# Fillers, load waits and the order of a few steps in a two-layer hybrid diffusion step

## The reference, cut to what matters

```
for l in range(2):
    sh1, sc1, ga1, sh2, sc2, ga2 = split(silu(cond) @ mod_w[l] + mod_b[l], 6)   # context and latent rows
    h = rms_norm(x, norm1_g[l]) * (1 + sc1) + sh1
    o = even_mixer(h) if l == 0 else odd_mixer(h)       # odd: Fourier mixer || 12-head latent attention
    x = x + ga1 * o
    h = rms_norm(x, norm2_g[l]) * (1 + sc2) + sh2
    g = argmax(group logits); e1, e2 = top2(expert logits within group g)
    x = x + ga2 * sum over e1, e2 of gate_e * (silu(h @ w1[e]) * (h @ w3[e])) @ w2[e]
y = rms_norm(x, final_norm_g)
# attention, per head: p = softmax(scale * (q_nope k_nope + q_pe k_pe)); out = p @ v
```

## Time and profile before

| | us |
|---|---|
| median of 3 runs (lowest, highest) | 779.63 (778.14, 781.07) |
| the profiled execution, whole | 773.11 |
| its span, first to last instruction | 771.3 |

### The profile page before, as it was taken

How to read it: one execution, slowest core, us unless ns; L and a number is a source line. 1 busy time by engine, 2 the same in 40 slices (tenths; PEclk the granted TensorE clock), 3 DMA queues, 4 the chain that set the end, 5 groups by cost and what they waited for, 6 DMA issues and landing times.

```text
span 771.3 us, 9539 instructions
## 1 busy us (share of the span) xinstructions
PE 694.5 (90%) x3655; PEld 388.2 (50%) x3655; DVE 244.7 (32%) x519; ACT 142.1 (18%) x290; POOL 170.8 (22%) x227
## 2 busy tenths in 40 slices
PE   1789999999999999799899998899799899999991
PEld 0335444554555665456445454355445556666650
DVE  0201212221155323223641323455221742323246
ACT  2101000000121212112121211355111121212211
POOL 5001011011331222212100210367404212222212
PEclk9899999999997999999989999999899899999996
DMA  9999999399356999996590582824410969979933
GB/s 329 393 359 308 400 386 365 110 419 425 165 204 250 400 419 421 420 421 249 199 410 8 207 357 110 332 105 157 144 55 28 358 259 416 419 302 423 384 136 131
DMA packets 53208, 219.46 MB, mean 285 GB/s; under 512 B 13774, under 2 KB 20942, under 8 KB 33969
## 3 DMA queue, kind: packets, MB, share of 16 engines
q1 hardware_dynamic: 31520, 178.59, 58.0%
q0 software_dynamic: 9664, 23.41, 8.1%
q10 hardware_dynamic: 11984, 16.92, 6.2%
HBM read 206.53 MB, written 20.68 MB: 295 GB/s over the span
## 4 chain that ended last, share of the span: by engine, by line
PE 69%; DMA 16%; DVE 6%; SPq 3%; issue 2%; ACT 2%; POOL 1%; ACTq 0%; POOLq 0%; DVEq 0%
PE ps L1371 12%; PE ps L1286 11%; PE ps L1444 8%; DMA pool<-in_mod_w 6%; DMA pool<-h_rows,of_now 5%; PE ps L1396 5%; PE ps L1480 5%; PE ps L1223 5%; DMA pool<-in_moe_w 4%; PE ps L1461 3%; PE ps L1612 2%; PE ps L1540 2%; PE ps L1358 2%; PE ps L1327 2%; SPq L383 2%
## 5 line engine op out<-in xcount | busy, mean ns | idle before, releaser
L1371 PE MATMUL ps<-pool 128*64 128x256 f32 x928 | 107.8, 390 | 3.6 <-issue 2.8
L1371 PEld LDWEIGHTS ps<-pool 128*64 128x64 f32 x928 | 77.4, 141 | 36.3 <-issue 13.5
L1286 PE MATMUL ps<-pool,turned 128*128 128x512 f32 x192 | 84.6, 595 | 0.0
L1223 PE MATMUL ps<-pool,cs 128*32 128x512 f32 x384 | 48.8, 636 | 19.8 <-DMA pool<-in_mod_w 10.8
L1444 PE MATMUL ps<-turned,pool 128*128 128x384 f32 x192 | 64.8, 492 | 0.0
L1396 PE MATMUL ps<-pool 128*64 128x512 f32 x240 | 54.8, 597 | 2.9 <-DMA pool<-in_moe_w 2.0
L1286 PEld LDWEIGHTS ps<-pool,turned 128*128 128x128 f32 x192 | 35.7, 190 | 41.3 <-issue 41.1
L1444 PEld LDWEIGHTS ps<-turned,pool 128*128 128x128 f32 x192 | 36.8, 196 | 30.4 <-issue 8.9
L543 POOL TENSOR_SCALAR pool<-pool 128x384 f32<-128x384 f32 (+1 forms) x36 | 36.6, 1031 | 59.3 <-DVE pool L1153 59.1
L958 DVE SCALAR_TENSOR_TENSOR pool<-ps,pool 128x256 f32<-128x256 f32 x20 | 9.7, 484 | 120.7 <-PE ps L1371 120.7
L413 POOL TENSOR_SCALAR rstd<-ss 128x1 f32<-128x1 f32 x24 | 9.6, 398 | 156.8 <-ACT xn L579 124.6
(11 more groups left out here) (243 smaller groups left out, 899.0 us busy)
## 6 DMA issues: line engine op xcount, KB each, us to landing
pool<-in_moe_w SPq DMA_DIRECT2D x72, 1024.0 KB, 16.5
pool<-in_mod_w SPq DMA_DIRECT2D x24, 2048.0 KB, 10.9
turned<-in_moe_w SPq DMA_DIRECT2D x18, 1024.0 KB, 14.4
pool<-in_ev_w_in SPq DMA_DIRECT2D x6, 1024.0 KB, 19.9
y_rows<-pool ACTq DMA_DIRECT2D x8, 768.0 KB, 20.3
xn<-in_moe_w SPq DMA_DIRECT2D x6, 1024.0 KB, 16.8
pool<-y_rows ACTq DMA_DIRECT2D x12, 512.0 KB, 6.5
pool<-in_ev_w_in SPq DMA_DIRECT2D x2, 2048.0 KB, 22.0
```

Of the source, the lines that this page charges most:

```text
L1223: ins = mm(ps[32 * j:32 * j + 32, 7, :], cs32[:, 2 * part + c, :], w[:, c, j * 512:(j + 1) * 512], start=part + c == 0, stop=part + c == 4)
L1286: ins = mm(ps[:, 2 * t + n, :], yT[:, k, t * P:(t + 1) * P], weight(parts[k // 4], 4, D)[:, k % 4, n * 512:n * 512 + 512], start=k == 0, s ...
L1371: ins = mm(ps[m, k, 0:DE], hTe.rearrange("p (c n) -> p c n", c=DC)[:, cc, m], w[e][:, cc, :], start=cc == 0, stop=cc == DC - 1)
```

## The change

Six edits. `rank_tokens` runs a third filler of 256 columns; `first_rows` starts with one of 256, and one of 384 columns stands between the first rows and their turning. The eighth weight load of an expert phase waits for both halves of the first rows' matmuls (`first_mm`) in place of the first gather; its other two waits stay. The four modulation quarters of layer 1's third part move from behind `head_q(1)` to behind the values' matmuls, ahead of the first keys, and DVE's `mod_rows(1, 2)` moves ahead of `head_q(0)`. ScalarE runs one exponential of 64 elements behind the first keys' copies (it writes a place that is overwritten later). Heads 0 and 11 are scaled by VectorE, right behind their reciprocals, and the other ten by GpSimd as before.

```diff
--- before.py
+++ after.py
@@ -232,7 +232,7 @@
             waits, fills = [], list(count)
             for s in order:
                 used = {}
-                for o in (owner[s], owner[s + 1]) if s < NSLOT else ((("router_mm", 3 * (l + 1)), ("h_rows", 16 * TILES * (l + 1)), (f"L{l}_gathered", 16))[0:s - NSLOT + 1]):
+                for o in (owner[s], owner[s + 1]) if s < NSLOT else ((("router_mm", 3 * (l + 1)), ("h_rows", 16 * TILES * (l + 1)), ("first_mm", 2 * l + 2))[0:s - NSLOT + 1]):
                     used[o[:-1]] = max(used.get(o[:-1], 0), o[-1])
                 waits.append(used)
             for n in range(3 * PAIRS):
@@ -537,7 +537,7 @@
             put_mods(1, 1)
             take_columns(1, 1, (1,))
             take_gate(1, 0)
-            for h in range(NH):
+            for h in range(1, NH - 1):
                 gps.wait_ge(S("pinv"), h + 1)
                 for t in range(TILES):
                     ins = nc.gpsimd.tensor_scalar(probs(h, t), probs(h, t), pinv[:, h % 2, t:t + 1], None, ALU.mult)
@@ -713,6 +713,8 @@
                 a_.activation(prT[h % 2][:, 0:512], ps[:, 4, :], ACT.Copy).then_inc(S("pT_act"), 1)
 
             k_pair(0)
+            act.wait_ge(S("kT"), 1)
+            ch.link(a_.activation(psum_of[0:NOPE, 1, 2:3], kT[0:NOPE, 0, 0:1], ACT.Exp, scale=0.0))
             act.wait_ge(S("new_kv"), 32)
             for h in range(NH):
 
@@ -1151,6 +1153,13 @@
                 if h >= 2:
                     dve.wait_ge(S("probs_even"), h - 1)
                 v_.reciprocal(pinv[:, h % 2], psum_of[:, h % 2]).then_inc(S("pinv"), 1)
+                if h in (0, NH - 1):
+                    dve.wait_ge(S("pinv"), h + 1)
+                    if h:
+                        dve.wait_ge(S("probs_even"), h)
+                    for t in range(TILES):
+                        ins = v_.tensor_scalar(probs(h, t), probs(h, t), pinv[:, h % 2, t:t + 1], None, ALU.mult)
+                    ins.then_inc(S("probs_even"), 1)
 
             def probs_out(h):
 
@@ -1175,10 +1184,10 @@
                 link(ins)
                 v_.tensor_scalar(nmax[:, h % 2], nmax[:, h % 2], -SCALE, None, ALU.mult).then_inc(S("nmax"), 1)
 
+            mod_rows(1, 2)
             head_q(0)
             head_maxima(0)
             head_q(1)
-            mod_rows(1, 2)
             for h in range(NH):
                 head_sums(h)
                 if h + 1 < NH:
@@ -1299,14 +1308,14 @@
                 turn_raw(l, 2)
                 router(l, 2)
 
-            def keep_clock(n, bank):
-
-                for _ in range(n):
-                    mm(ps[:, bank, :], ident, cst[:, C_CS2:C_CS2 + 512], start=True, stop=True)
+            def keep_clock(bank, *widths):
+
+                for n in widths:
+                    mm(ps[:, bank, 0:n], ident, cst[:, C_CS2:C_CS2 + n], start=True, stop=True)
 
             def rank_tokens(l):
 
-                keep_clock(2, 1)
+                keep_clock(1, 512, 512, 256)
                 pe.wait_ge(*L(l, "mask", 1))
                 ones = cst[:, C_ONE:C_ONE + 1].broadcast_to((P, P))
                 for s in range(TILES):
@@ -1318,6 +1327,7 @@
 
             def first_rows(l):
 
+                keep_clock(1, 256)
                 pe.wait_ge(S("h_made"), 2 * (l + 1))
                 pe.wait_ge(*L(l, "first_hot", 1))
                 for half in range(2):
@@ -1398,6 +1408,7 @@
                     ins.then_inc(S(f"L{l}_down_mm"), 1)
 
                 first_rows(l)
+                keep_clock(1, 384)
                 pe.wait_ge(S("first_act"), l + 1)
                 pe.wait_ge(S("first_dve"), l + 1)
                 turn_rows(range(DC), ys)
@@ -1553,6 +1564,9 @@
                         ins = mm(ps[:, (6, 3)[kt % 2] + n, 0:(h1 - h0) * VD], kvT[:, cc, kt * P:(kt + 1) * P],
                                  ukv[:, cc, h0:h1, NOPE:NOPE + VD], start=cc == 0, stop=cc == 1)
                 ins.then_inc(S("v2_mm"), 1)
+            pe.wait_ge(S("vv"), 3)
+            for part in range(4):
+                mod_part(1, 2, part)
             pe.wait_ge(S("q_rot"), 1)
             pe.wait_ge(S("q_out"), 3)
             pe.wait_ge(S("vv"), 4)
@@ -1619,8 +1633,6 @@
             head_q(0)
             head_scores(0)
             head_q(1)
-            for part in range(4):
-                mod_part(1, 2, part)
             pe.wait_ge(S("mod_row"), 6)
             for h in range(NH):
                 if h + 1 < NH:
```

## The result

The changed kernel takes 764.61 us (median of 4 runs, 763.49 to 772.87) against 778.88 for the kernel before (4 runs): ratio 0.984, 95% interval 0.981 to 0.988. Two later sets of the same kernel on other chips gave 0.9835 and 0.9837. By these ratios 12.2 to 12.9 us are gained; the forecast was 12.0. The two medians lie 14.3 apart: the run of 772.87 counts in the ratio and not in the median.

A forecast was written before the change was run, and what follows sets the result against it. PE's chain of stages bounds the kernel, with waits and half-clock stretches. Terms 7.8 (layer 0), 1.5 (layer 1), 0.95 (modulation) and 1.7 (scales) sum to 12.0 us: 767.6 on the median, chance 0.50, range 764.5 to 771, 8 in 10 761.5 to 775.

The forecast's parts named there:

- signs named: Trace signs, among them: eighth load by 241, ninth near 247, layer 0 weight waits under 1 us, first ups near 6.9.
- The early fill: Layer 0's expert weights come 4.9 or 7.8 us earlier; 7.8 us gained there, first step's clock included; layer 1 gains 0.
- rival 3: Gathers take over in every step of layer 0 and the clock isn't held: 0 gained there, 777.8 us, chance 0.10.
- 2.9 us of clock in layer 0: Fillers hold full clock in layer 0's first expert step: ups 6.91 instead of 9.79 us, counted inside the 7.8.
- the stretch before them ... I take 0: First rows' clock: narrow matmuls before them remain, so no gain was counted; 1.7 us a layer kept as an end.
- Layer 1: 1.5 forecast: Fillers hold the clock in layer 1's first step: ups 6.91 instead of 8.44 us, 1.5 gained; the fill gives 0.
- rival 2: The clock holds everywhere, first rows gaining 1.7 us in each layer: 16.65 us gained, 763.0 us, chance 0.13.
- rival 4: Layer 0's gather lands late beside the early eighth load, so PE waits: 4.25 us lost, 783.9 us, chance 0.07.
- Modulation quarters: Start of attention: the 64 modulation matmuls directly behind the values bring head 1's scores 0.95 us sooner; ends 0 and 1.5.
- The cover lost: Head 0's softmax no longer lies under the 64 modulation matmuls; counted as 0.
- Tail scales: Attention's end, head 11 scaled by VectorE: 0.9 us sooner plus 0.8 of clock, 1.7; ends 0.9 and 3.3 (clock never falls).
- Rival 1: The fillers don't hold the clock: layer 0 gains 4.9, layer 1 0, 6.75 us in all, 772.9 us, chance 0.20.

The follow-up runs named there:

- e0: The changed kernel run again without edit, on another chip: median 766.26 us, ratio 0.9835 to the kernel before.
- e12: The changed kernel run a third time without edit: median 765.59 us, ratio 0.9837 to the kernel before.
- e6: The kernel before with the early eighth weight load in both layers as the only edit: median 773.54 us, ratio 0.9897 to the kernel before.
- e5: The changed kernel with the early eighth load in layer 0 alone; in layer 1 it waits for the gather: ratio 0.9781 to the kernel before, 0.9855 when repeated.
- e3: The changed kernel with the last modulation quarters and VectorE's two adds back behind the first scores: median 766.88 us, ratio 0.9834 to the kernel before.
- e2: The changed kernel with each layer's eighth weight load waiting for the gather again: median 770.07 us, ratio 0.9892 to the kernel before.

## Why the prediction was right, and where not

The number was met in part by luck. The terms were read from one execution and added to 12.0, which made 761.1 of it and, scaled, 767.6 of the median. The three profiles of the changed kernel took 763.69, 766.57 and 766.28, so against that execution the gain was 6.5 to 9.4 and the forecast too large; against the median, 764.61, it was too small. Between the two lies the clock: the execution was at 0.962 and the timed runs at 0.954 in the mean, so that they had more to win by the clock than the rows showed. The sum had no term for the 1.3 us lost before the values, nor for the end stage, which is 0.5 to 2.0 longer than before in the three profiles.

Of the signs named, three were missed by little: the eighth load was issued at 241.79 and not by 241, the ninth at 249.35 and not near 247, and PE's waits on weights between 300 and 340 were 1.5 us and not under 1.

**The early fill: right, a little small.** The third store is the last that the eighth load waits for, as forecast (by 0.2 us here, by 2.7 and 3.0 in e0 and e12):

```profile
241.79 0.33 SPq L383 DMA_DIRECT2D turned<-in_moe_w  x1
...
245.65 7.13 PE L1381 MATMUL ps<-pool 128*64 128x256 f32 x64 [0.24 <-issue]
247.00 1.46 POOL L423 DMA_INDIRECT pool<-h_rows,of_rows  x1 [10.17 <-DVE of_rows L942]
249.35 4.28 SPq L383 DMA_DIRECT2D pool<-in_moe_w  x4
```

The lead of the weight stream was put at 4.9 without the clock; in e6, counted from the router's last matmuls, the last packet of the ninth load ends 5.3 sooner (33.4 instead of 38.7) and layer 0 gains 5.74. Gathers did not take over (rival 3): PE waited for them there for 1.0 us in e6, and for 0.4, 2.3 and 1.1 in the three executions of the changed kernel, where 1.2 had been charged.

**The step that failed: 2.9 us of clock in layer 0.** The fillers do hold the clock of the first ups, which gained 9.79 - 7.13 = 2.7. But "the stretch before them ... I take 0" was wrong, to both sides. In the profiled execution the fall is now in the ranks and the first rows, and the ups start 2.1 us later, counted from the router's last matmuls, so the gap shrank by 0.7. That is one of two such profiles: over layer 0's routing and first step the clock is at half for 13.65 us in the kernel before and in e6, and with all added fillers for 13.65 in two profiles of nine (the other is e5) and for 3.4 to 6.8 in seven. Yet even where the gap shrank by 3.5 (e12), the sum of layer 0 gained 7.0 against 5.74 for the fill alone: the weight stream ends last there, and an earlier first step waits for it (PE's waits on weights in layer 0 are 2.8 us in e12 and 0.7 in e6). Layer 0 gained 5.9, 6.8 and 7.0 in three executions, not 7.8; and 1.3 and 1.4 of it were given back before the values in two of them, 0.7 and 1.2 of that because more of the first in-projection matmuls run at half clock (8.58 and 9.05 in the chain instead of 7.87).

**Layer 1: 1.5 forecast, 0.9, 0.2 and 2.0 measured, by another way.** The clock gained more than forecast (gap 1.9 to 3.1 shorter, since the first rows ran at 5.40, too: rival 2's term). But rival 4's wait came, in layer 1: the ups end so early that the gather beside the eighth load lands behind them, 8.52 us under way instead of 3.9 before:

```profile
610.31 0.33 SPq L383 DMA_DIRECT2D turned<-in_moe_w  x1
...
613.50 1.53 POOL L423 DMA_INDIRECT pool<-h_rows,of_rows  x1 [7.80 <-DVE of_rows L942]
...
622.07 0.71 PE L1368 MATMUL ps<-cst,pool 128*128 128x128 f32 x4 [2.92 <-DMA pool<-h_rows,of_rows]
```

The text set "the fill gives 0 there"; with the clock held it costs 2.4 to 3.0 at this place. In layer 0 the eighth load had 5.2 us of lead over the gather, which landed in 4.7, before the ups ended; in layer 1 it had 3.2. In all seven profiles with the early load in layer 1 the lead is 2.2 to 3.4 us where the first rows there took 5.39 and 4.7 to 5.8 where they took 7.0, so the clock that was won goes with this wait: rivals 2 and 4 are not independent. But the lead isn't all. With the early load, 4.1 us of it or more gave landings of 4.6 to 5.1 in both layers; 2.2 to 3.4 us gave 5.2 to 6.1 in layer 0, where PE then waited 0.4 at most, and 7.1 to 8.6 in layer 1. What more holds the gather up in layer 1 stays open. The Trainium skill ("DMA: Bandwidth & Descriptors", "Queues, rings and completion order") has a completion written only after its engine's earlier writes; the 8.52 beside the load and the 3.9 of e5 without it agree.

**Modulation quarters: 0.95 forecast, 1.10 measured,** in every execution with the edit, 0 without (e3, e6). The named lines came: modulation straight behind the values, keys without idle time.

```profile
471.14 7.07 PE L1232 MATMUL ps<-pool,cs 128*32 128x512 f32 x64
478.15 1.94 PE L1609 MATMUL ps<-turned,pool 128*64 128x512 f32 x8
```

The cover lost was costed at nothing. In two of eleven profiles with the new order the clock fell between head 0's scores and head 2's (486.2 in e0, 488.6 in e2), in none of three with the old; that is a hint, not shown.

**Tail scales: 1.7 forecast, 3.40, 1.71 and 1.78 measured.** The transposes came 1.07 sooner (0.9 forecast). The rest is the clock: the upper end, that it never falls, came in the profiled execution; in two others a fall elsewhere in the heads took 1.6 back. So a smaller layer 0 was made up for in part by a larger tail.

**Rival 1** is refuted by the ups: 7.13 wherever all the fillers are in. The rule beside it in the prediction (the Trainium skill, "TensorE: Matmul & The Clock Gate", "Why this matters for your kernels", drops after long gaps without PE work) does not cover what decided here: the falls came behind stretches with short gaps (PE busy for 2.20 of 3.40 us in the earlier trace rows, for 2.82 of 3.41 in e0 ahead of 233.66), and filler columns removed one of them.

**Still open:** the end stage takes 23.75 to 26.3 us, and 24.20 to 25.73 in the same kernel. The last read of the result rows is 4.96 us under way in the changed kernel, 6.83 in e5:

```profile
735.10 4.96 DMA pool<-y_rows
```

```profile
734.83 6.83 DMA pool<-y_rows
```

What it shares the engines with was not tried. Nor was the early dummy exponential taken out alone: the trace shows ScalarE's 1.28 us of table load at 481.35, ahead of head 0's exponentials, where it had stood right before them; what that is worth by itself no run shows.

## What to carry to other kernels

Where a stage has two limits (here PE's clock and the weight stream), the gains of two edits don't add: work out for each which one ends last when the other is done. A load that is brought forward into an empty DMA stretch needs a lead over the small gather behind it that PE will wait for, or it trades one wait for another. Before a sum is built on one profiled execution, compare its time and its clock with the timed runs of the same kernel. A filler is judged by the whole routing stretch, since it can move a clock fall to earlier work as well as remove it.

## What the runs showed of the hardware

The granted clock falls at different places in different executions of one program: layer 0's routing had 13.65 us at half clock in one, twice 3.4 in another, 6.8 in a third. The first gather of layer 1, which lands in 3.4 to 4.0 us with no load issued shortly ahead of it, took 7.1 to 8.6 with 2 MB of weights issued 2.2 to 3.4 us ahead, and 4.6 to 4.9 with these 4.7 us or more ahead. VectorE scales a head in a third of GpSimd's time (heads 10 and 11 in the changed kernel):

```profile
534.11 3.05 POOL L543 TENSOR_SCALAR pool<-pool 128x128 f32<-128x128 f32 x3 [1.70 <-DVE pool L1155]
```

```profile
537.26 0.95 DVE L1161 TENSOR_SCALAR pool<-pool 128x128 f32<-128x128 f32 x3
```
